# First block: two PSUM bank assignments, a mask laid into a table, and the order of the mix chunks

## What is computed

```python
def hybrid_mixer(x, w_in, ...):
    proj = x @ w_in
    qa, ka, va, qb, kb, vb, gb, gc, hc, gates = split(proj)
    oa = diff_attention(qa, ka, va, lam, pos)       # 4 heads, two softmaxes each, rope
    ya = rms_norm(oa, subln_g) * (1.0 - lam_init)
    yb = neighbourhood_attention(qb, kb, vb, rpb)   # 8 heads, bias rpb, window of 16 columns
    yc = gb * dwconv(gc * hc, sc_conv_w)
    g = sigmoid(gates)
    merged = g[0] * (ya @ w_branch[0]) + g[1] * (yb @ w_branch[1]) + g[2] * (yc @ w_branch[2])
    return merged @ w_mix_out
# layer: x = ln(alpha*x + hybrid_mixer(x)); x = ln(alpha*x + memory_cross_attention(x, mem)); x = ln(alpha*x + conv_ffn(x))
```

## Time and profile before

| | |
|---|---|
| median of 3 runs | 2728.57 us |
| the profiled execution | 2725.55 us, of which the profile spans 2723.6 us |
| PE busy | 98% of the span, 18229 matmuls and transposes |
| DVE, ACT, POOL busy | 77%, 62%, 3% |
| granted TensorE clock, mean | 0.988 of full |
| first block | 0 to about 1180 us: layer 0 to about 597 us, layer 1 from there |

### The profile page before, as it was taken

The page is one execution under the profiler, slowest core; times in us unless marked ns, Lnnn a source line. Parts: engine busy times, 40 slices in busy tenths (PEclk is TensorE's granted clock), DMA queues, the critical chain, the costliest instruction groups (busy, mean ns, idle before and its releaser), DMA issues.

```text
span 2723.6 us, 42449 instructions
## 1 busy us (share of the span) xinstructions
PE 2656.3 (98%) x18229; PEld 2437.7 (90%) x18229; DVE 2097.2 (77%) x2086; ACT 1681.7 (62%) x1813; POOL 69.8 (3%) x120
## 2 busy tenths in 40 slices
PE   8999999999999999999999999999999999999998
PEld 7989999999899999989999999788888888888886
DVE  7677658877677568867677666789898989988897
ACT  5455546654555456554678644677777777777775
POOL 1000000001000000000011000000000000000000
PEclk9999999999999999999999999999999999999999
DMA  7545557746445467542799633699999989998995
GB/s 238 186 132 173 161 184 261 263 136 205 140 140 186 153 234 263 201 129 94 255 317 316 198 109 116 271 375 357 349 366 364 366 340 377 351 385 341 359 373 192
DMA packets 303618, 677.66 MB, mean 249 GB/s; under 512 B 16672, under 2 KB 237120, under 8 KB 260416
## 3 DMA queue, kind: packets, MB, share of 16 engines
q1 hardware_dynamic: 288080, 617.67, 62.6%
q0 software_dynamic: 15344, 57.21, 6.3%
HBM read 671.68 MB, written 1.05 MB: 247 GB/s over the span
## 4 chain that ended last, share of the span: by engine, by line
PE 84%; DVE 8%; ACT 5%; issue 2%; DMA 1%; POOL 0%; SPq 0%; ACTq 0%; DVEq 0%
PE bank L581 80%; DVE ring_low L1498 2%; ACT w_hi L2153 1%; PE bank L1247 1%; DVE ring_low L1376 1%; PE bank L666 1%; PE bank L683 1%; PE bank L624 1%; DVE ring_tail L1453 1%; PE bank L725 0%; ACT ring_low L2167 0%; ACT ring_tail L2239 0%; ACT xs_hi L2223 0%; DMA ring_head<-in_w_mix_out 0%; DMA ring_head<-in_ffn_w_in 0%
## 5 line engine op out<-in xcount | busy, mean ns | idle before, releaser
L1981 DVE TENSOR_TENSOR ew_lo<-ring_head,ew_hi 128x2048 fp32r<-128x2048 f32 x336 | 758.9, 2287 | 47.7 <-ACT ew_hi L2530 47.6
L2530 ACT CAST ew_hi<-ring_head 128x2048 fp32r<-128x2048 f32 x336 | 642.2, 1916 | 224.7 <-PE bank L581 224.5
L581 PE MATMUL bank<-xs_hi,ring_low 128*128 128x256 f32 (+1 forms) x2608 | 513.2, 284 | 3.1 <-DVE ring_low L1376 2.9
L581 PEld LDWEIGHTS bank<-xs_hi,ring_low 128*128 128x128 f32 (+1 forms) x2608 | 416.2, 191 | 10.4 <-issue 6.0
L581 PE MATMUL bank<-ew_hi,gathered_hi 128*128 128x512 f32 x896 | 353.8, 395 | 0.0
L581 PE MATMUL bank<-ew_hi,gathered_lo 128*128 128x512 f32 x896 | 349.7, 390 | 0.0
L581 PE MATMUL bank<-ew_lo,gathered_hi 128*128 128x512 f32 x896 | 349.3, 390 | 0.0
L581 PE MATMUL bank<-x_hi,w_hi 128*128 128x256 f32 x1152 | 318.1, 282 | 3.3 <-ACT x_hi L2231 2.6
L581 PE MATMUL bank<-x_hi,ring_low 128*128 128x256 f32 x1152 | 314.8, 279 | 0.0
L1498 DVE TENSOR_TENSOR ring_low<-ring_head,w_hi 128x2048 fp32r<-128x2048 f32 x105 | 239.7, 2289 | 88.2 <-ACT w_hi L2153 88.2
L581 PE MATMUL bank<-x_lo,w_hi 128*128 128x256 f32 x1080 | 294.9, 279 | 0.0
(11 more groups left out here) (444 smaller groups left out, 5346.0 us busy)
## 6 DMA issues: line engine op xcount, KB each, us to landing
ring_head<-in_moe_w_gate SPq DMA_DIRECT2D x112, 1024.0 KB, 7.2
ring_head<-in_moe_w_up SPq DMA_DIRECT2D x112, 1024.0 KB, 7.0
ring_head<-in_moe_w_down SPq DMA_DIRECT2D x112, 1024.0 KB, 7.0
ring_head<-in_w_in SPq DMA_DIRECT2D x82, 1024.0 KB, 5.2
ring_tail<-in_ada_w POOLq DMA_DIRECT2D x48, 1024.0 KB, 9.0
ring_head<-in_ffn_w_in SPq DMA_DIRECT2D x44, 1024.0 KB, 7.2
ring_head<-in_ffn_w_out SPq DMA_DIRECT2D x22, 1024.0 KB, 8.8
ring_head<-in_xa_kv SPq DMA_DIRECT2D x16, 1024.0 KB, 5.5
```

The costliest lines, as they stand in the source:

```text
L581: ins = nc.tensor.matmul(out, lhsT, rhs, start=start, stop=stop, **kw)
L1981: v.tensor_tensor(ew_lo[:, h, :], ring(c % 6), ew_hi[:, h, :].bitcast(F32), ALU.subtract).then_inc(w_used[c % 6], 1)
L2530: a.copy(ew_hi[:, (e * len(PARTS) + c) % DEPTH_HI, :], ring(c % 6)).then_inc(f.count(part_hi), 1)
```

## The change

It makes six edits, in both layers unless a layer is named.

1. Score step 1 alone writes banks 2 and 3 in place of 0 and 1.
2. The sums of squares of step 10 go to banks 2 and 3 in place of 4 and 5.
3. The window mask is laid into the bias table on the host; DVE's addition L1589 is gone.
4. `three` gets `high_first`: it waits for the chunk's high part alone, issues all high x high and high x low products, waits for the low part ahead of the first p = 2 product, and issues those; `chunk_done` is raised by the first p = 2 product (for chunk 42 still by the last p < 2). It is used for chunks 42 to 47, and for chunks 1 and 2 in layer 0.
5. The transposes inside chunks 43 to 45 move to before (1, 4, 0), the 25th matmul of the new order, those inside 46 and 47 to before (1, 0, 0), the 17th.
6. DVE makes chunk 42's low part after the gate product and sum of the eleventh half-size chunk, chunk 43's after those of the twelfth and `mix_low(3)`, chunk 44's after the first residual, 45's after the second, 46's and 47's after the third.

```diff
+        def score_bank(u):
+            return 2 if u == 1 else 0
...
-            def three(b, i, x, k=KD, turned=False, order=None, before=None, mixer=False, early=False):
+            def three(b, i, x, k=KD, turned=False, order=None, before=None, mixer=False, early=False, high_first=False):
...
-                if early:
+                if high_first and order is None:
+                    order = passes(range(k))
+                if early or high_first:
                     pe.wait_ge(chunk_hi, count + 1)
...
                 released = max(n for n, (p, t, j) in enumerate(order) if p < 2)
+                first_low = min(n for n, (p, t, j) in enumerate(order) if p == 2)
+                if high_first:
+                    released = max(released, first_low)
                 for n, (p, t, j) in enumerate(order):
+                    if high_first and n == first_low:
+                        pe.wait_ge(chunk_lo, count + 1)
...
-                            three(4 if c == 5 else c % 4, c, xs, turned=c in (4, 5))
+                            three(4 if c == 5 else c % 4, c, xs, turned=c in (4, 5), high_first=l == 0 and c < 3)
...
-                            if u == 0:
-                                taken(0)
-                            open_bank(1)
+                            if u < 2:
+                                taken(2 * u)
+                            open_bank(score_bank(u) + 1)
...
-                                b = 4 + h // 2
+                                b = 2 + h // 2
...
-                    three(0, 42, xs, order=passes(range(6)) + passes((6, 7)), before=late(src_lo, 8 * l + 7, 6))
+                    three(0, 42, xs, order=passes(range(6)) + passes((6, 7)), before=late(src_lo, 8 * l + 7, 6), high_first=True)
...
-                        three(n, 42 + n, xs, before=piece_within(n, mix_banks[0]))
+                        three(n, 42 + n, xs, before=piece_within(n, mix_banks[0], (1, 4, 0)), high_first=True)
...
-                        if (p, t, j) == (0, 4, 0):
+                        if (p, t, j) == (1, 0, 0):
                             taken(3)
                             piece_turned(3, mix_banks[0])
...
-                    three(2, 46, mem, before=last_piece)
-                    three(3, 47, mem, before=back_within)
+                    three(2, 46, mem, before=last_piece, high_first=True)
+                    three(3, 47, mem, before=back_within, high_first=True)
...
-                            wide = bias.rearrange("p h j c -> p (h j) c")
-                            v.tensor_tensor(wide, wide, spread(const[:, C_WIN:C_WIN + 64], 48), ALU.add).then_inc(f.count(vector_step), 1)
...
-                            low_part(l, 33 + c)
+                            if c != 9:
+                                low_part(l, 33 + c - c // 10)
...
                         if n < 3:
-                            low_part(l, 45 + n)
+                            low_part(l, 44 + n)
+                        if n == 2:
+                            low_part(l, 47)
...
-                                take(4 + j, ka[:, 2 * j:2 * j + 2, :])
+                                eng.wait_ge(bank_full[2 + j], f.now(bank_full[2 + j]) + 4 + j)
+                                a.copy(ka[:, 2 * j:2 * j + 2, :], tiles(bank[2 + j][:, :], 2)).then_inc(bank_free[2 + j], 1)
```

More of the change, by code:

```diff
@@ L111 @@
     "src_ready": 5, "std_ready": 3, "y_turned": 12, "x_turned": 12, "xn_first": 6, "xn_second": 6, "sub_squares": 1, "sub_std": 1, "summed": 4, "x_half": 3, "up_full0": 6,
-    "up_full1": 5, "var_ready": 3, "vector_step": 182, "w_loaded0": 240, "w_loaded1": 240, "w_loaded3": 256,
+    "up_full1": 5, "var_ready": 3, "vector_step": 181, "w_loaded0": 240, "w_loaded1": 240, "w_loaded3": 256,
     "w_loaded4": 256, "w_used0": 21, "w_used1": 21, "w_used2": 6, "w_used3": 21, "w_used4": 21, "w_used5": 5,
@@ L127 @@
     "src_ready": 5, "std_ready": 3, "y_turned": 12, "x_turned": 12, "xn_first": 6, "xn_second": 6, "sub_squares": 1, "sub_std": 1, "summed": 4, "x_half": 2, "up_full0": 6,
-    "up_full1": 5, "var_ready": 3, "vector_step": 178, "w_loaded0": 240, "w_loaded1": 240, "w_loaded3": 256,
+    "up_full1": 5, "var_ready": 3, "vector_step": 177, "w_loaded0": 240, "w_loaded1": 240, "w_loaded3": 256,
     "w_loaded4": 256, "w_used0": 21, "w_used1": 21, "w_used2": 6, "w_used3": 21, "w_used4": 21, "w_used5": 5,
@@ L837, in _ @@
                             a, t, qt = u // 8, u // 2 % 4, u % 2
-                            if u == 0:
-                                taken(0)
-                            open_bank(1)
+                            if u < 2:
+                                taken(2 * u)
+                            open_bank(score_bank(u) + 1)
                             for m in range(2):
-                                head = slice(64 * m, 64 * m + 64)
-                                mm(bank[m][:, 0:TOK], (qa, qb)[a][head, t, qt * P:(qt + 1) * P], (ka, kb)[a][head, t, :],
-                                   True, True, bank_full[1] if m else None)
+                                head, b = slice(64 * m, 64 * m + 64), score_bank(u) + m
+                                mm(bank[b][:, 0:TOK], (qa, qb)[a][head, t, qt * P:(qt + 1) * P], (ka, kb)[a][head, t, :],
+                                   True, True, bank_full[b] if m else None)
                         if u:
@@ L888, in _, with piece_within @@
                     pe.wait_ge(src_lo, 8 * l + 6)
-                    three(0, 42, xs, order=passes(range(6)) + passes((6, 7)), before=late(src_lo, 8 * l + 7, 6))
-                    def piece_within(n, into):
+                    three(0, 42, xs, order=passes(range(6)) + passes((6, 7)), before=late(src_lo, 8 * l + 7, 6), high_first=True)
+                    def piece_within(n, into, at=(0, 4, 0)):
                         def before(p, t, j):
-                            if (p, t, j) == (0, 4, 0):
+                            if (p, t, j) == at:
                                 if n == 1:
@@ L1465, in peaks @@
                 b = u % 2
-                own = 1 if apart else b
-                found = banks[:, 0:2, 0:TOK] if apart else pairs(b)
+                first = score_bank(u)
+                own = first + 1 if apart else b
+                found = banks[:, first:first + 2, 0:TOK] if apart else pairs(b)
                 dve.wait_ge(bank_full[own], f.next(bank_full[own]))
@@ L1554, in _ @@
                         if c == 5:
-                            f.bump(bank_full[4], 11)
-                            f.bump(bank_free[4], 11)
+                            f.bump(bank_full[4], 10)
+                            f.bump(bank_free[4], 10)
                         if c < 4:
@@ L1587, in _ @@
                             dve.wait_ge(bias_in, f.next(bias_in, 64))
-                            wide = bias.rearrange("p h j c -> p (h j) c")
-                            v.tensor_tensor(wide, wide, spread(const[:, C_WIN:C_WIN + 64], 48), ALU.add).then_inc(f.count(vector_step), 1)
                         if u == 10:
+                            for b in (2, 3):
+                                f.bump(bank_full[b])
+                                f.bump(bank_free[b])
                             dve.wait_ge(bank_free[7], f.now(bank_free[7]) + 6)
@@ L2627, in constants @@
     c[:, C_DIAG:C_DIAG + P] = (j <= i) & (j // 64 == i // 64)
-    q, k = np.arange(64)[:, None], np.arange(64)[None, :]
-    start = np.clip(q - 8, 0, 48)
-    c[:, C_WIN:C_WIN + 64] = np.tile(np.where((k >= start) & (k < start + 16), 0.0, NEG), (2, 1))
     for m in range(2):
@@ L2704, in layout @@
     shifts = 63 - np.arange(64)[:, None] + np.arange(64)[None, :]
-    arrays["bias"] = np.concatenate([rpb[:, :, 1 - s:7 - s][..., shifts].transpose(0, 3, 1, 2, 4).reshape(DEPTH, 64, -1)
-                                     for s in range(2)], axis=1)
+    q, k = np.arange(64)[:, None], np.arange(64)[None, :]
+    first = np.clip(q - 8, 0, 48)
+    window = (k >= first) & (k < first + 16)
+    arrays["bias"] = np.concatenate([np.where(window, rpb[:, :, 1 - s:7 - s][..., shifts], NEG).transpose(0, 3, 1, 2, 4).reshape(DEPTH, 64, -1)
+                                     for s in range(2)], axis=1).astype(np.float32)
     return {n: np.ascontiguousarray(a) for n, a in arrays.items()}
```

## The result

| | before | after |
|---|---|---|
| median, four runs each | 2728.60 us (2726.53 to 2730.01) | 2705.42 us (2702.48 to 2707.11) |
| the profiled execution | 2725.55 us, span 2723.6 | 2706.59 us, span 2704.7 |

The ratio is 0.9917 (0.9901 to 0.9933). The medians differ by 23.2 us and the two profiled executions by 19.0; the forecast was 21.1 us and 2707.5. A later set of five runs of the changed kernel had its median at 2705.63 (2699.81 to 2707.51), 21.0 us under before in the same set.

A forecast was written before the change was run, and what follows sets the result against it. PE was taken as the bound: 84% of the chain that ended last, 98% busy. Gains of 9.4 us a layer, 18.8 for two, plus 2.35 at the start made 21.1 us: median 2728.57 to 2707.5 us, range 2702 to 2714.

The forecast's parts named there:

- Chunks 1 and 2: Start of layer 0: PE starts chunk 1 at about 19.42 instead of 21.77, behind ACT's high part; 2.35 us gained.
- Score step 1: Second score step: PE's 0.82 us wait for DVE to empty banks 0 and 1 goes; 0.85 us a layer.
- Mask: Transposes after the mask addition: they follow the last matmul by one pitch instead of 0.85 us; 0.73 us a layer.
- Squares and clock: Step 10: PE's wait for ACT's copy goes, 1.9 us a layer, and the low clock behind it, 1.5 us.
- the prediction's second rival: Low-clock stretches behind step 10 have another cause and stay, or come elsewhere: 3.0 us lost, 2710.5 to 2712 us; chance 0.14.
- Mix: Chunks 42 to 47: waits for low parts, group 3's sum and the residual go; 4.4 us a layer, bounds 2.5 to 4.9.
- (a): Chunk 42: high first lets PE start at 251.84 instead of 253.52; 1.69 us gained.
- (b): Group 3's sum in chunk 42: the 1.90 us wait goes but for about 0.1 us.
- (c): Chunk 43's transposes: the 1.19 us wait for the residual goes.
- (d): Chunk 47: sixteen transposes come after 16 matmuls instead of 12, delaying chunk 49; 0.47 us given back.
- The new bound of the rival: Chunks 42 to 47: a late load replaces DVE, half or all of 8.8 us given back, 2712 to 2716; chance 0.12.
- The allowance of 3 us either way: Whole kernel: other short clock dips may come or go when the schedule moves; likeliest case 2703 to 2712 us.

The follow-up runs named there:

- mask only: The kernel before with only DVE's mask addition L1589 removed and the mask put in the host's table; 2722.18 us, one execution.
- squares only: The kernel before with only the sums of squares of step 10 moved to banks 2 and 3; 2718.54 us, ratio 0.9975.
- mix only: The kernel before with only chunks 42 to 47 changed: high first, later transposes, DVE's new order; 2716.03 us, ratio 0.9963.
- scores only: The kernel before with only score step 1 moved to banks 2 and 3; 2725.52 us, one execution.
- chunks 1 and 2 only: The kernel before with only chunks 1 and 2 of layer 0 high first; 2721.69 us, one execution.
- the table's last row: The kernel before run once more, unchanged, for a second profile; 2728.46 us.

## Why the prediction was right, and where it was not

**The sum.** 21.1 us were forecast; the profile shows 21.3 at the end of block one (0.2 of them from an earlier chunk 0), 19.0 at the end, the medians 23.2 and 21.0. Layer 1 was to begin 11.7 us earlier and does so by 12.0.

**Chunks 1 and 2**: 2.35 forecast, 2.4 alone. ACT became the releaser, as said.

**Score step 1**: 0.85 forecast. PE's wait from start to start was 1.20 us against 0.21 without, so 0.99, and 0.16 came back at the first transposes. The warning that the cover there was thin, 0.13 us, was right to 0.03.

**Mask**: 0.73 forecast, 0.8 measured, in after and in mask only, and nothing late next.

**Squares and clock**: 1.9 + 1.5 forecast, 3.4 measured in both layers of after and of squares only. The wait is the sure part, the clock is not. Six profiles have the wait in place. Before (twice) and mix only show the dip in all 6 layers (in layer 0 the same program up to there; in layer 1 mix only is changed ahead of it and dips too). Mask only, scores only, and chunks 1 and 2 only, each changed ahead of step 10, show it in none of 6. The profiles without the wait (after twice and five experiments) show it in 0 of 14. So the wait is needed for the dip but is not enough for it, as the prediction's second rival held from the waits that left the clock alone. For the kernel before the 1.5 us were there in both profiles; whether its other executions have them is not shown, and no program was seen both with and without the dip at step 10, so whether the execution or the changed program ahead of it decides stays open. I had not seen that chunk 1's wait of 2.86 us carries the same risk: a dip behind it in 2 of its 6 profiles (3.4 and 6.8 us long), none in the seven where it is shortened. There all six run the same program up to the wait, so it is the execution that decides. What differs between such executions I did not settle.

The Trainium skill, TensorE: Matmul & The Clock Gate, section "Loop structure matters more than you think", has it that a copy out of PSUM between matmuls does not cool PE, in a loop whose next matmuls follow at once. In step 10 PE stood idle for 1.81 us until the copy was done, so the page does not speak of this case, and the prediction read too much into it when it let the dip stay by it. The dip went in all 14 layers without the wait.

**Mix**: 4.4 a layer forecast, 4.8 and 4.8 in after, 4.5 and 4.8 alone. (a) Chunk 42 follows at once. (b) The 0.1 us left over for group 3's sum isn't seen: the sum is ready 0.07 us before it is wanted, so this cover is as thin as I had it. (c) Chunk 43's transposes do not wait. (d) The 0.47 us given back is there: in front of chunk 49 two starts lie 0.84 us apart instead of 0.37, and with the transposes moved ahead in chunk 47 that wait is gone. But I had entered it as a price of the design, where one position or one more `high_first` takes it away. The new bound of the rival shows too: ACT waits 3.00 to 4.71 us for the loads of chunks 46 to 48, but PE does not wait for ACT; the 17 us between issue and use were enough.

**The rivals.** High first does not cost pitch: 0.116 us a matmul. Block two did take 2.4 us back in the profile, and the same kernel run again (the table's last row) lost as much there. The allowance of 3 us either way was thus of the right size, but for another reason than the one given: it was to cover dips of the clock that shift, and 2.0 us of the loss lie in a stretch at granted clock 1.00 where PE's pace is 1% slower. That it came out in size is luck. The dips that did shift, one lost near 1325 us of before and one gained near 1577, make up the small rest.

## What to carry to other kernels

Where a weight is split in two parts, issue all products of the first part ahead of those of the second: PE then waits for one engine rather than two in a row. At the kernel's start this alone gave 2.4 us. In the mix chunks it gave next to nothing until the other engine's order was changed with it, so write down for each product the time at which it is wanted and let the second engine work in that order. A wait like those of 1.8 to 3.5 us here may cost twice, by the clock as well, and one profile doesn't say whether it does. Two profiles of one kernel differed by 2.9 us here, so the worth of an edit of 1 us is read between two markers on either side of it, not from the whole time.

## What the runs showed of the hardware that I had not expected

The same wait of 1.81 us at step 10 was followed by 3.4 us at 1.2 GHz in 6 layers of 12: in all 6 of the kernel before and mix only, in none of the 6 of three kernels changed ahead of it. A wait of 2.9 us, with the same program ahead of it in all six executions, was followed by the lower clock in 2 of them; waits of 3.5 and 3.4 us were followed by it both times.

At a granted clock of 1.00 and without any wait, the same kernel started 1717 matmuls in 200 us in one execution and 1700 in another, 1% fewer.

The way from PE's last matmul over one DVE instruction of 0.69 us and back to PE's transposes took 1.06 us from start to start, and an idle DVE made it no shorter.
